# The end of a decoder layer: the down projection's last four units by token tile, and its last tile finished in two halves of the features

## What is computed

```
x   = x + mixed @ w_o
h   = rms_norm(x, norm_ffn_g)
g, u = split(h @ w_ffn_in)                  # 2 x 2816 columns
x   = x + (silu(g) * u) @ w_ffn_out         # down projection, 2816 -> 1024
out = x * rsqrt(mean(x * x) + 1e-6) * norm_final_g
```

## Time and profile before

| | us |
|---|---|
| median of 3 runs | 859.2 (858.9 to 860.84) |
| the profiled execution | 860.79 |
| its span | 858.6 |
| PE busy | 835.2 (97%) |
| DVE busy | 412.1 (48%) |
| ACT busy | 332.6 (39%) |
| granted clock, mean | 0.998 |

### The profile page before, as it was taken

How to read it: one execution, slowest core, us unless ns; L and a number is a source line. 1 busy time by engine, 2 the same in 40 slices (tenths; PEclk the granted TensorE clock), 3 DMA queues, 4 the chain that set the end, 5 groups by cost and what they waited for, 6 DMA issues and landing times.

```text
span 858.6 us, 12164 instructions
## 1 busy us (share of the span) xinstructions
PE 835.2 (97%) x4633; PEld 672.2 (78%) x4633; DVE 412.1 (48%) x596; ACT 332.6 (39%) x508; POOL 117.7 (14%) x124
## 2 busy tenths in 40 slices
PE   5999999999999999999999999999999999999996
PEld 4677767788888777777888898888888888888885
DVE  5479769452453544544662654444444444222215
ACT  6568332232323533435432444444444444211122
POOL 3053870221222201100320000000000000000000
PEclk9999999999999999999999999999999999999999
DMA  6421341421125122123344143333333332222222
GB/s 190 138 74 49 76 145 50 111 56 34 38 67 167 50 75 74 50 74 99 98 161 157 31 142 98 98 98 95 95 93 93 92 101 92 99 97 97 98 74 98
DMA packets 122426, 79.97 MB, mean 93 GB/s; under 512 B 15041, under 2 KB 110322, under 8 KB 122386
## 3 DMA queue, kind: packets, MB, share of 16 engines
q1 hardware_dynamic: 122194, 79.39, 31.0%
q0 software_dynamic: 192, 0.02, 0.0%
HBM read 74.15 MB, written 5.24 MB: 92 GB/s over the span
## 4 chain that ended last, share of the span: by engine, by line
PE 90%; DVE 5%; ACT 3%; DMA 1%; issue 1%; POOL 0%; SPq 0%; ACTq 0%; POOLq 0%; DVEq 0%
PE PS L1526 26%; PE PS L1528 25%; PE PS L1527 25%; PE PS L1622 2%; PE PS L1876 1%; PE PS L1887 1%; PE PS L1899 1%; DVE sq L1196 1%; DVE w_lo L1122 1%; PE PS L1729 1%; PE PS L1768 1%; PE PS L1769 1%; PE PS L1747 1%; PE PS L1807 1%; DMA xt<-in_x_dram 1%
## 5 line engine op out<-in xcount | busy, mean ns | idle before, releaser
L1526 PE MATMUL PS<-hT_hi,w_hi 128*128 128x512 f32 (+2 forms) x688 | 270.7, 393 | 3.4 <-DVE hT_lo L1146 1.3
L1528 PE MATMUL PS<-hT_hi,w_lo 128*128 128x512 f32 (+2 forms) x688 | 263.2, 382 | 0.0
L1527 PE MATMUL PS<-hT_lo,w_hi 128*128 128x512 f32 (+2 forms) x688 | 263.1, 382 | 0.0
L1122 DVE TENSOR_TENSOR w_lo<-wraw,w_hi 128x1024 fp32r<-128x1024 f32 (+1 forms) x125 | 163.2, 1307 | 154.0 <-ACT w_hi L767 151.7
L767 ACT ACTIVATE w_hi<-wraw 128x1024 fp32r<-128x1024 f32 (+1 forms) x125 | 131.3, 1050 | 130.0 <-PE PS L1528 106.3
L1526 PEld LDWEIGHTS PS<-hT_hi,w_hi 128*128 128x128 f32 (+1 forms) x688 | 128.6, 187 | 36.7 <-issue 10.2
L1528 PEld LDWEIGHTS PS<-hT_hi,w_lo 128*128 128x128 f32 (+1 forms) x688 | 128.7, 187 | 26.5
L1527 PEld LDWEIGHTS PS<-hT_lo,w_hi 128*128 128x128 f32 (+1 forms) x688 | 128.8, 187 | 24.6 <-issue 1.0
L1526 PE MATMUL PS<-w_hi,act_hi 128*128 128x512 f32 x176 | 68.5, 389 | 0.0
L1528 PE MATMUL PS<-w_hi,act_lo 128*128 128x512 f32 x176 | 68.5, 389 | 0.0
L1527 PE MATMUL PS<-w_lo,act_hi 128*128 128x512 f32 x176 | 68.5, 389 | 0.0
(11 more groups left out here) (241 smaller groups left out, 1040.3 us busy)
## 6 DMA issues: line engine op xcount, KB each, us to landing
wraw<-in_w_ffn_in_dram SPq DMA_DIRECT2D x88, 256.0 KB, 3.0
wraw<-in_w_in_dram SPq DMA_DIRECT2D x82, 256.0 KB, 3.1
wraw<-in_w_ffn_out_dram SPq DMA_DIRECT2D x44, 256.0 KB, 2.8
wraw<-in_w_o_dram SPq DMA_DIRECT2D x16, 256.0 KB, 3.0
xt<-in_x_dram SPq DMA_DIRECT2D x4, 512.0 KB, 5.3
qk_scratch<-stage SPq DMA_DIRECT2D x8, 256.0 KB, 3.0
qkT<-qk_scratch SPq DMA_DIRECT2D x4, 512.0 KB, 4.4
wraw<-in_w_up_a_dram SPq DMA_DIRECT2D x8, 256.0 KB, 2.9
```

The lines of the kernel that those rows point to most:

```text
L1122: dve.tensor_tensor(w_lo[:, q, 0:n], wraw[:, s, 0:n], w_hi[:, q, 0:n].bitcast(F32), ALU.subtract)\
L1526: pe.matmul(out_, a_hi, b_hi, start=start, stop=False)
L1527: pe.matmul(out_, a_hi, b_lo, start=False, stop=False)
L1528: return pe.matmul(out_, a_lo, b_hi, start=False, stop=stop)
```

## The change

The down projection gets a constant of its own, LAST_DOWN = 4: the first 18 units run unit by unit, the last four tile by tile. `down` is cut into `down_half`, for one half of the features. For the first three tiles both halves are computed per unit as before. For the last tile (t = 1) the half of the features is the outer loop: its four units for half 0, `z_mm_out`, then its four units for half 1, `z_mm_out`.

DVE now finishes each of the first three tiles directly behind its sum. For the last tile it sums half 0; waits for its squares and makes the mean square of it; sums half 1; multiplies half 1 by `gfin` into a new buffer `xg3`; adds the mean square of half 1; takes the reciprocal and scales half 0. ACT squares each half, takes the root, scales half 1 of `xg3` by a Copy with a per-row scale, and stores half 1 by a DMA of its own. SP stores half 0. So the last store is two of 256 KB, with rows of 2 KB, from two queues.

```diff
@@ -79,6 +79,7 @@
 N_SHIFT = 15
 WO_ORDER = [2, 3, 0, 1]
 LAST = 3
+LAST_DOWN = 4
 RKV_TILE = [4, 5, 6, 7, 0, 1, 2, 3, 8, 9, 10, 11]
 VB_BANK = [7, 0, 5, 6]
 FILL_BANK = [7, 3]
@@ -133,6 +134,7 @@
         omu = sb("omu", [P, 16])
         ss = sb("ss", [P, 3, TT])
         rstd = sb("rstd", [P, 3, TT])
+        last_ss = sb("last_ss", [P, 2])
         warm = sb("warm", [P, 4])
         at[0] = (at[0] + ROW - 1) // ROW * ROW
         hT_hi = sb("hT_hi", [P, KD, T], F32R)
@@ -284,6 +286,7 @@
         x3 = sb("x3", [P, TT, D])
         fin = sb("fin", [P, TT, D])
         junk3 = sb("junk3", [P, D])
+        xg3 = sb("xg3", [P, D // 2])
 
 
         w_loaded = [sem(f"w_loaded{i}") for i in range(NRAW)]
@@ -414,6 +417,9 @@
         x3_ready = sem("x3_ready")
         gfin_loaded = sem("gfin_loaded")
         fin_ready = sem("fin_ready")
+        fin_last = sem("fin_last")
+        gx_ready = sem("gx_ready")
+        half_ms = sem("half_ms")
         out_done = sem("out_done")
 
         def pc(name, i=0, n=None):
@@ -586,10 +592,13 @@
             load_rows(U_FO + FT - 1, U_FO + FT - 1, w_ffn_out, (FT - 1) * P)
             sp.wait_ge(actlo_ready, FT)
             sp.dma_start(gfin[:], norm_final_g.partition_broadcast(P)).then_inc(gfin_loaded, 16)
-            for n, t in enumerate(WO_ORDER):
+            for n, t in enumerate(WO_ORDER[:-1]):
                 sp.wait_ge(fin_ready, n + 1)
                 sp.dma_start(outd[:, t, :], fin[:, t, :]).then_inc(out_done, 16)
-            sp.wait_ge(out_done, 16 * TT)
+            t = WO_ORDER[-1]
+            sp.wait_ge(fin_ready, TT)
+            sp.dma_start(outd[:, t, 0:D // 2], fin[:, t, 0:D // 2]).then_inc(out_done, 16)
+            sp.wait_ge(out_done, 16 * (TT + 1))
 
 
         @block.gpsimd
@@ -1099,9 +1108,21 @@
             for u in range(U_FO + LEAD + (FT - LEAD) // 4 * 4, N_UNITS):
                 split_hi(u, u)
             act.activation(warm[:, 3:4], warm[:, 0:1], ACT.Sqrt)
-            for n, t in enumerate(WO_ORDER):
+            for n, t in enumerate(WO_ORDER[:-1]):
                 squares(x3, junk3, 2, n, (x3_ready, n + 1), t)
                 std(2 * TT + n)
+            t = WO_ORDER[-1]
+            for h in range(2):
+                hc = slice(h * D // 2, (h + 1) * D // 2)
+                act.wait_ge(x3_ready, TT + h)
+                act.activation(junk3[:, hc], x3[:, t, hc], ACT.Square, accum_out=last_ss[:, h:h + 1])\
+                   .then_inc(ss_ready, 1)
+            std(3 * TT - 1)
+            act.wait_ge(rstd_ready, 3 * TT)
+            act.wait_ge(gx_ready, 1)
+            act.activation(fin[:, t, D // 2:D], xg3[:], ACT.Copy, scale=rstd[:, 2, TT - 1:TT]).then_inc(fin_last, 1)
+            act.wait_ge(fin_last, 1)
+            act.dma_start(outd[:, t, D // 2:D], fin[:, t, D // 2:D]).then_inc(out_done, 16)
 
 
         @block.vector
@@ -1509,14 +1530,35 @@
                 dve.scalar_tensor_tensor(out=fin[:, t, :], in0=x3[:, t, :], scalar=rstd[:, 2, n:n + 1],
                                          in1=gfin[:], op0=ALU.mult, op1=ALU.mult).then_inc(fin_ready, 1)
 
-            for n, t in enumerate(WO_ORDER):
+            for n, t in enumerate(WO_ORDER[:-1]):
                 dve.wait_ge(z_mm_out, n + 1)
                 dve.tensor_tensor(x3[:, t, :].rearrange("p (a b) -> p a b", a=2),
                                   x2[:, t, :].rearrange("p (a b) -> p a b", a=2), PS[:, 2 * t:2 * t + 2, :],
                                   ALU.add).then_inc(x3_ready, 1)
-                if n:
-                    finish(n - 1, WO_ORDER[n - 1])
-            finish(TT - 1, WO_ORDER[TT - 1])
+                finish(n, t)
+
+            t = WO_ORDER[-1]
+            half = [slice(h * D // 2, (h + 1) * D // 2) for h in range(2)]
+            s = ss[:, 2, TT - 1:TT]
+
+            def last_sum(h):
+                dve.wait_ge(z_mm_out, TT + h)
+                dve.tensor_tensor(x3[:, t, half[h]], x2[:, t, half[h]], PS[:, 2 * t + h, :], ALU.add)\
+                   .then_inc(x3_ready, 1)
+
+            last_sum(0)
+            dve.wait_ge(ss_ready, 3 * TT)
+            dve.tensor_scalar(s, last_ss[:, 0:1], 1.0 / D, RMS_EPS, ALU.mult, ALU.add).then_inc(half_ms, 1)
+            last_sum(1)
+            dve.wait_ge(x3_ready, TT + 1)
+            dve.tensor_tensor(xg3[:], x3[:, t, half[1]], gfin[:, half[1]], ALU.mult).then_inc(gx_ready, 1)
+            dve.wait_ge(half_ms, 1)
+            dve.wait_ge(ss_ready, 3 * TT + 1)
+            dve.scalar_tensor_tensor(out=s, in0=last_ss[:, 1:2], scalar=1.0 / D, in1=s, op0=ALU.mult, op1=ALU.add)\
+               .then_inc(ms_ready, 1)
+            norm(None, None, 2, TT - 1)
+            dve.scalar_tensor_tensor(out=fin[:, t, half[0]], in0=x3[:, t, half[0]], scalar=rstd[:, 2, TT - 1:TT],
+                                     in1=gfin[:, half[0]], op0=ALU.mult, op1=ALU.mult).then_inc(fin_ready, 1)
 
 
         @block.tensor
@@ -2020,16 +2062,18 @@
                         project(u, f, 2 * j + g).then_inc(w_used, 1)
 
 
-            def down(k, t, start, stop):
+            def down_half(k, t, h, start, stop):
                 q = (U_FO + k) % NSPL
                 ts = slice(t * P, (t + 1) * P)
-                for h in range(2):
-                    w = slice(512 * h, 512 * h + 512)
-                    ins = three(PS[:, 2 * t + h, :], act_hi[:, k, ts], act_lo[:, k, ts], w_hi[:, q, w], w_lo[:, q, w],
-                                start, stop)
-                return ins
-
-            for k in range(FT - LAST):
+                w = slice(512 * h, 512 * h + 512)
+                return three(PS[:, 2 * t + h, :], act_hi[:, k, ts], act_lo[:, k, ts], w_hi[:, q, w], w_lo[:, q, w],
+                             start, stop)
+
+            def down(k, t, start, stop):
+                down_half(k, t, 0, start, stop)
+                return down_half(k, t, 1, start, stop)
+
+            for k in range(FT - LAST_DOWN):
                 take(U_FO + k)
                 pe.wait_ge(actlo_ready, 1 if k == 0 else FT)
                 for t in WO_ORDER:
@@ -2037,10 +2081,14 @@
                         pe.wait_ge(prod_ready, FT + 2)
                     ins = down(k, t, k == 0, False)
                 ins.then_inc(w_used, 1)
-            for t in WO_ORDER:
-                for k in range(FT - LAST, FT):
+            for t in WO_ORDER[:-1]:
+                for k in range(FT - LAST_DOWN, FT):
                     take(U_FO + k)
                     ins = down(k, t, False, k == FT - 1)
+                ins.then_inc(z_mm_out, 1)
+            for h in range(2):
+                for k in range(FT - LAST_DOWN, FT):
+                    ins = down_half(k, WO_ORDER[-1], h, False, k == FT - 1)
                 ins.then_inc(z_mm_out, 1)
```

## The result

The median is 858.67 us over 15 runs (856.24 to 860.28), against 860.36 (858.78 to 862.48) for 15 runs of the kernel before in the same comparison: a difference of 1.69, or 0.20%. The ratio of the two kernels is 0.9976, with a 95% interval of 0.9966 to 0.9985, so 0.24% faster (0.15% to 0.34%). It isn't the quotient of the medians, but its interval holds the 0.20% too. The table of before gives 859.2, the median of three runs; over 15 runs the same kernel has 860.36, 1.16 more.

What follows compares the result with a forecast made beforehand. PE is busy nearly throughout, so only the 7.85 us after the last matmul could shrink: scalings end 1.57 us earlier, stores land in 2.85 instead of 2.6, so 1.3 off the 859.2 median gives 857.9 us, range 857.0 to 859.6.

Steps and rivals of the forecast that it cites:

- the sum itself: The forecast's main case, all terms added: median 857.9 us, own range 857.4 to 858.5, chance 0.60.
- the rival in which the gain is eaten on DVE: Half-0 sum starts only with the last matmul, end moves by 1.16 us: time 858.5 to 859.3, chance 0.15.
- The matmuls stay: Down projection on PE: same matmuls and spacing, last unit's weights in time with 1.7 us left, last sum can start at 850.78.
- Half-0 sum behind the third tile's scaling: Last tile on DVE: data there at 848.06, but queued behind that scaling, so the sum starts at 849.62.
- Half-1 sum behind the half mean square: Last tile on DVE: the sum starts at 851.20 instead of 850.78, a wait costing 0.42 us.
- The new tail: From the half-1 sum on: combined mean square 852.69, scalings from 853.32, ending by 854.07, 1.57 us earlier than before.
- The stores: Two 256 KB stores from SP and ACT at about 854.1, landing 2.85 us later at 856.95, against 858.27.
- The lower bound of 2.0: Landing time of the half stores if the halves didn't disturb each other: 1.4 + 0.6 us.
- the rival of early halves: Two last stores land 2.0 to 2.4 us after issue: gain 1.8 to 2.2, time 857.0 to 857.4, chance 0.15.
- ACT's queue: Rival at the last store: ACT's first DMA answers late, no gain from a landing of 4.2 us on, chance 0.06.
- Time outside the span: Around the span: profiled execution 860.79 against span 858.6; new span 857.3 gives time 859.5.
- within: Outcome between the edges 857.5 and 860.9 us, about 0.2% from no change: chance 0.67.

Runs made afterwards that it cites:

- e9: Changed kernel with three further ACT copies of 1024 columns ahead of the last unit's copy: tail 7.09 us, ratio 0.9998.
- e3: Changed kernel with three units of the down projection outside by tile (LAST_DOWN = 3) instead of four: tail 8.47 us, ratio 1.0005.
- e7: Changed kernel with DVE's half mean square and its wait moved behind the half-1 sum and the product with gfin: tail 6.48 us, ratio 0.9966.
- e6: Changed kernel with both half stores of the last tile issued by SP, one behind the other: tail 6.74 us, ratio 0.9975.
- e12: Kernel before with only the change's new semaphores and tiles declared, not used: time outside the span 2.13 us, ratio 1.0007.
- e10: Kernel before with the last tile's 512 KB store issued by ACT instead of SP: time outside the span 2.20 us, ratio 1.0005.
- e11: Kernel before with the last tile, scaled whole, stored in two halves from SP and ACT: tail 8.30 us, outside the span 2.19, ratio 1.0005.
- e2: Kernel before with each finish directly behind its own sum and four units outside by tile instead of three: tail 7.81 us, ratio 0.9997.
- e5: Changed kernel with the last tile stored by one 512 KB DMA from SP behind both scalings: tail 6.70 us, ratio 0.9970.
- e8: Changed kernel, half mean square behind the half-1 sum, no combined one; ACT's root takes scale 1/D and the half mean square as bias: tail 6.34 us, ratio 0.9977.
- e1: Kernel before with each finish directly behind its own sum, three units outside, no halves, one store: tail 8.32 us, ratio 0.9999.

## Why the prediction was right

The saving was forecast at 1.3 us and is 1.69 by the medians, and the steps in the tail came as forecast. The absolute number, 857.9, owes something to the width of the range: 858.67 lies within 857.0 to 859.6, but above the 857.4 to 858.5 that the sum itself was given, in the band of the rival in which the gain is eaten on DVE. That rival did not come true. The starting point was wrong: the median of three runs, 859.2, is 1.16 below that of 15. The base 1.16 higher and the saving 0.39 larger make the 0.77 between 857.9 and 858.67.

Each step of the sum is set beside the changed kernel's row less 1.08, the difference of the last matmuls.

- **The matmuls stay.** No gap after 829, the last unit's low part in time. The cover was put at 1.7 and is 1.48 (e9): I took the time at which the slot was released (829.04) plus three units, 18 matmuls, but the next matmul starts ahead of that release.
- **Half-0 sum behind the third tile's scaling.** Forecast 849.62; 850.69 - 1.08 = 849.61. In the rival of the eaten gain this sum waits for the third tile until the last matmul has run; that is so only in e3.
- **Half-1 sum behind the half mean square.** Forecast 851.20; 852.23 - 1.08 = 851.15. The price of that wait, 0.42 in the forecast, is 0.37 (e7).
- **The new tail.** Combined mean square 852.69 against 852.69, where two small errors cancel: the squares start 0.07 earlier than forecast, and from them to the mean square it is 0.83 instead of 0.76 (0.10 after the accumulator read, where the half mean square follows after 0.03). Both scalings from 853.32, against 853.32. The last one's end was to come 1.57 us earlier and does.
- **The stores.** Forecast 2.85 to landing; measured 2.7. Tail in all: 1.3 forecast, 1.48 measured. The lower bound of 2.0, put together as 1.4 + 0.6, is what the first half store of e6 takes, issued 0.38 ahead of the second; two issued together land at 2.5 and 2.7, and the last byte is early in neither, so the rival of early halves fell; ACT's queue answered in 2.5, not late.
- **Time outside the span.** The forecast carried it over unchanged from the profiled execution of before. It became 0.37 less, and beyond the 0.15 of the stores that is what the sum missed. It takes the change from 0.17% to 0.215% by the rows. The ratio has 0.24%, but its interval of 0.15% to 0.34% lies on both sides of the 0.2% that I had called the edge; so the runs don't decide between "within", which had 0.67, and "faster by over 0.2%", which had 0.25. What causes the 0.37 is open. Each by itself, it isn't the declarations (e12), the store from ACT (e10), the split store (e11), nor the order with the fourth unit (e2): it appears with the last tile worked in halves (1.74 in e3, whose tail is longer than before), 0.2 of it goes when ACT issues no DMA (e5, e6), and 0.13 when the root gets a bias (e8). No trace has a row there.

**Which part gives what**, in the end of the last scaling, taken in this order: order and four units 0.52 (e2), the halves on DVE and ACT a further 1.05 (4.76 to 3.71), the second queue and the split store nothing (e5, e6, e11). That the order without the fourth unit gives nothing (e1) and the halves without it lose (e3) shows that these aren't independent: DVE's work for a tile must be shorter than PE's step. The prediction added this work up for the third tile (845.34 to 849.69, 4.35) but didn't set it against PE's step. With four units outside nothing followed from that; with three the lateness would have been missed, as it was in the expectation for e1. The kernel before doesn't show it either: its DVE order had sum n + 1 ahead of finish n.

The kernel with the best ratio is e7, 0.9966. Its tail is 0.3 to 0.4 shorter than the changed kernel's by the rows; the two ratios' intervals overlap, so in time that isn't shown.

## What to carry to other kernels

A kernel whose last engine is full to the end can still be shortened behind it, but read the tail from the last matmul's start, not from the span, when the gain is smaller than the scatter of what comes before. Where a result is handed over tile by tile, compare the length of the consumer's whole chain for one tile with the producer's step: here 4.25 against 4.08 made a reordering worthless, and against 5.44 it paid. And on an engine that works its program off in order put no wait for a small result in front of larger work whose data is there first; here that cost 0.37 (e7).

## What was not expected of the hardware

- The time outside the span changes with the end of the program, cause open: 2.12 us before, 1.75 changed, 1.95 with the same halves and one store from SP, each within 0.1 or so over all runs of a kernel.
- A root of one column takes 0.20 us without a scale or a bias from a tile, and 0.29 with an immediate scale and a per-row bias (e8); which of the two costs the 0.09 wasn't separated.
- Two stores of 256 KB issued 0.38 apart on one queue land 2.0 and 2.2 after their issues (e6); two issued together on two queues 2.5 and 2.7 (2.4 and 2.6 in e11, 2.5 and 3.0 in e9); one of 512 KB 2.6.
